# Modulation vectors summed along rows of transposed weights, and four PSUM banks for the second chunk of a joined output stage

## What is computed

```python
sc, sc_ctx = jax.nn.silu(c), jax.nn.silu(c_ctx)
for i in range(DEPTH):                                  # 2 layers
    m  = (sc @ w_mod[i] + b_mod[i]).reshape(B, N_MOD, D_MODEL)[:, :, None, :]
    mc = (sc_ctx @ w_mod[i] + b_mod[i]).reshape(N_MOD, D_MODEL)
    shift_m, scale_m, gate_m, shift_f, scale_f, gate_f = [m[:, k] for k in range(N_MOD)]
    h = modulate(rmsnorm_2(x, g_pre_mix[i]), shift_m, scale_m)
    ...
```

## Time and profile before

| what | value |
|---|---|
| median of 3 executions | 3549.88 us (3549.67 to 3550.25) |
| profiled execution | span 3547.7 us from first to last instruction (its own time is not given apart; the median lies 2.2 us above this span) |
| PE, PEld (weight load) | 3348.4 us (94%), 2947.4 us (83%) |
| DVE | 2189.7 us (62%) |
| ACT, POOL | 1734.8 us (49%), 1370.2 us (39%) |
| granted PE clock, mean | 0.971 of full speed |
| DMA | 337.33 MB, mean 95 GB/s |

### The profile page before, as it was taken

One profiled execution on the slowest core, in us unless ns is written; L12 is line 12 of the kernel. 1 busy time (PEld: TensorE's weight loads), 2 busy tenths in 40 slices (PEclk: granted clock), 3 DMA queues, 4 the chain that ended last, 5 costly groups with the idle time before them and its releaser, 6 DMA issues. The chain is left out here.

```text
span 3547.7 us, 57878 instructions
## 1 busy us (share of the span) xinstructions
PE 3348.4 (94%) x18421; PEld 2947.4 (83%) x18421; DVE 2189.7 (62%) x4470; ACT 1734.8 (49%) x4097; POOL 1370.2 (39%) x1781
## 2 busy tenths in 40 slices
PE   8899798999999999797999989999999889999999
PEld 7899587999999997686899868888788768888787
DVE  7467775555677776335888476656436775665335
ACT  2578123767777772333566363333334653333233
POOL 5465333555666773313222524444102224444000
PEclk9999899999999998898999989999999989999999
DMA  6211745111222114400000122222355212221464
GB/s 264 82 31 46 286 186 183 42 35 49 62 64 66 57 61 175 138 1 30 1 0 0 54 107 77 89 79 81 119 176 193 83 65 83 77 89 71 145 198 161
DMA packets 104142, 337.33 MB, mean 95 GB/s; under 512 B 11617, under 2 KB 40209, under 8 KB 90258
## 3 DMA queue, kind: packets, MB, share of 16 engines
q1 hardware_dynamic: 103954, 335.07, 27.3%
HBM read 273.13 MB, written 61.10 MB: 94 GB/s over the span
## 5 line engine op out<-in xcount | busy, mean ns | idle before, releaser
L2128 PE MATMUL ps<-down_high,hidden_high 128*128 128x512 f32 x688 | 269.3, 391 | 6.9 <-DVE hidden_low L2029 4.4
L2129 PE MATMUL ps<-down_low,hidden_high 128*128 128x512 f32 x688 | 268.0, 390 | 0.0
L2130 PE MATMUL ps<-down_high,hidden_low 128*128 128x512 f32 x688 | 268.0, 389 | 0.0
L2027 DVE TENSOR_TENSOR down_low<-down_raw,down_high 128x1024 fp32r<-128x1024 f32 x86 | 108.7, 1264 | 247.6 <-ACT down_high L1942 247.5
L2108 PE MATMUL ps<-columns_combined,up_high_even 128*128 128x512 f32 x616 | 242.8, 394 | 13.0 <-DVE columns_combined L2427 5.9
L2109 PE MATMUL ps<-columns_combined,up_high_even 128*128 128x512 f32 x616 | 241.8, 393 | 0.0
L2110 PE MATMUL ps<-columns_combined,up_low_even 128*128 128x512 f32 x616 | 241.6, 392 | 0.0
L2108 PE MATMUL ps<-columns_combined,up_high_odd 128*128 128x512 f32 x616 | 239.6, 389 | 0.0
L2109 PE MATMUL ps<-columns_combined,up_high_odd 128*128 128x512 f32 x616 | 239.6, 389 | 0.0
L2110 PE MATMUL ps<-columns_combined,up_low_odd 128*128 128x512 f32 x616 | 239.6, 389 | 0.0
L1137 ACT ACTIVATE masked_then_probs<-masked_then_probs,unit_rows 128x256 f32<-128x256 f32 (+1 forms) x512 | 229.2, 450 | 9.1 <-DVE unit_rows L1216 4.3
(11 more groups left out here) (440 smaller groups left out, 10131.9 us busy)
## 6 DMA issues: line engine op xcount, KB each, us to landing
up_raw<-in_w_up SPq DMA_DIRECT2D x44, 1024.0 KB, 4.8
down_raw<-in_w_down SPq DMA_DIRECT2D x88, 512.0 KB, 3.6
mod_weights_b<-in_w_mod SPq DMA_DIRECT2D x32, 1024.0 KB, 6.0
hidden_columns<-hidden SPq DMA_DIRECT2D x44, 512.0 KB, 2.6
hidden_columns<-hidden_columns SPq DMA_DIRECT2D x88, 256.0 KB, 3.9
w_raw<-in_w_in_b SPq DMA_DIRECT2D x24, 768.0 KB, 4.6
mod_weights<-in_w_mod SPq DMA_DIRECT2D x8, 2048.0 KB, 11.9
x_kept<-x SPq DMA_DIRECT2D x24, 512.0 KB, 2.7
```

The lines of the kernel that those rows point to most:

```text
L2128: nc.tensor.matmul(out, h_hi[to][:, t], down_hi[to][:, cols], start=begin, stop=False)
L2129: nc.tensor.matmul(out, h_hi[to][:, t], down_lo[to][:, cols], start=False, stop=False)
L2130: last = nc.tensor.matmul(out, h_lo[to][:, t], down_hi[to][:, cols], start=False, stop=(end and to == self.slot(h, f, s)))
```

## The change

- `w_mod` is laid out transposed: block b holds, for 128 output features on the partitions, the weights of all 1024 inputs in a row. There are 96 blocks of 128x1024. silu(c) and silu(c_ctx) are rows of 1024, copied to all partitions by a DMA (`c_rows`), with the SiLU on ACT (two operations of 128x1024 in the opening). The row of silu(c) stays in SBUF at a fixed place (`C_ROW_AT`).
- One `tensor_tensor_reduce` of DVE multiplies a block by the row and sums it into one column of `mod_sums`; its 128x1024 output (`unread`, two of them in turn) is not used. No transposes, no reductions, no wait on the operation just before, but on the one before that.
- Loads are pairs of blocks, 1 MB, three slots in the ring in every stage.
- Blocks by stage: opening 24, of which 16 for both vectors (40 operations); joined stage 40; second mixer's output product 32.
- Joined stage: `EARLY` = 16 blocks before `add(0, m)`, one block behind each tile of chunk 1 (at the end of the tile's work, behind `low`), the last 16 after `low(TILES - 1)`. Chunk 1 uses four banks (`m % 4`), and the gate columns' product waits for the additions only.
- `mixer_out` is written out by itself in place of `project`; x is loaded at its start and not after the split of the tokens. The two groups of products stand before the additions of chunk 0 and before those of chunk 1.

```diff
+class Modulation:
+    SLOTS = 3
...
+    def load(self, sp, q):
+        if q >= self.SLOTS:
+            sp.wait_ge(core.mod_sums.sem, core.mod_sums.at(self.before(2 * (q - self.SLOTS + 1))))
+        at = self.first + 2 * q
+        sp.dma_start(self.raw[:, q % self.SLOTS], self.w[at:at + 2].rearrange("b p n -> p b n")).then_inc(self.landed[q % self.SLOTS].sem, 16)
+
+    def products(self, dve, a, b):
...
+            for v in range(2 if n < self.both else 1):
+                i = self.before(n) + v
+                if i >= 2:
+                    dve.wait_ge(core.mod_sums.sem, core.mod_sums.at(i - 1))
+                dve.tensor_tensor_reduce(out=self.unread[:, i % 2], in0=self.raw[:, q % self.SLOTS, n % 2], in1=self.rows[v], scale=1.0, scalar=0.0,
+                                         op0=ALU.mult, op1=ALU.add, accum_out=self.sums[:, v, n:n + 1]).then_inc(core.mod_sums.sem, 1)
```

In `opening`:

```diff
-                side.sync(sp, 0)
+                for n in range(2):
+                    sp.dma_start(modulation.rows[n], I["c_rows"][n].partition_broadcast(P)).then_inc(core.beside0.sem, 16)
+                for q in range(3):
+                    modulation.load(sp, q)
                 sp.dma_start(X[:], I["x"][0].rearrange("(m p) n -> p m n", p=P)).then_inc(core.post_row.sem, 16)
...
-                side.sync(sp, 1)
+                for q in range(3, 8):
+                    modulation.load(sp, q)
                 for c in range(CHUNKS):
...
+                    for q in range(8, 0 if c else modulation.pairs):
+                        modulation.load(sp, q)
...
+                act.wait_ge(core.beside0.sem, core.beside0.at(32))
+                for n in range(2):
+                    act.activation(modulation.rows[n], modulation.rows[n], ACT.Silu).then_inc(core.expo.sem, 1)
...
-                side.pe(lambda m: pe.wait_ge(core.acc_used_act.sem, core.acc_used_act.at((CHUNKS - 1) * TILES + m + 1)))
```

In `out_and_gate`:

```diff
                 sp.dma_start(X[:], old).then_inc(core.ready2.sem, 16)
-                for q in range(SLOTS, 9):
-                    mod(q)
+                mods(3, 6)
                 split_done(KT)
                 load(3)
-                mod(9)
-                mod(10)
+                mods(6, 9)
...
-                    dve.tensor_tensor(X[:, m, cols], ps[:, m if c == 0 else m % 2, :], X[:, m, cols], ALU.add).then_inc(core.acc_used_dve.sem, 1)
+                    dve.tensor_tensor(X[:, m, cols], ps[:, m if c == 0 else m % 4, :], X[:, m, cols], ALU.add).then_inc(core.acc_used_dve.sem, 1)
...
-                early = 48
-                products(0, early)
+                modulation.products(dve, 0, EARLY)
...
                     add(1, m)
-                    if m >= 2:
-                        reduced(0, m - 2, 3 - m % 2)
-                    products(early + 2 * m, early + 2 * m + 2)
                     normed(m)
                     if m:
                         low(m - 1)
-                reduced(0, MODS - 2, 3)
+                    modulation.products(dve, EARLY + m, EARLY + m + 1)
                 low(TILES - 1)
-                reduced(0, MODS - 1, 4)
-                shifted(0)
-                products(KT * MODS, 2 * KT * MODS)
-                for n in range(MODS):
-                    reduced(1, n, n)
-                shifted(1)
+                modulation.products(dve, EARLY + TILES, modulation.blocks)
+                modulation.shift(dve)
...
-                    pe.wait_ge(core.acc_used_dve.sem, core.acc_used_dve.at(m + 1 if m < 2 else TILES + m - 1))
+                    pe.wait_ge(core.acc_used_dve.sem, core.acc_used_dve.at(m + 1 if m < 4 else TILES + m - 3))
...
-                            if k == 0 and m in (0, 1):
-                                pe.wait_ge(core.acc_used_dve.sem, core.acc_used_dve.at(2 * TILES - 1 + m))
-                            if k == 0 and m in (2, 3, 4):
-                                pe.wait_ge(core.mod_reduced.sem, core.mod_reduced.at(m + 4))
+                            if k == 0 and m < 4:
+                                pe.wait_ge(core.acc_used_dve.sem, core.acc_used_dve.at(TILES + m + 5))
```

The new `mixer_out`, DVE's part of it:

```diff
+                modulation.products(dve, 0, EARLY)
+                dve.wait_ge(core.ready2.sem, core.ready2.at(16))
+                add(0)
+                modulation.products(dve, EARLY, modulation.blocks)
+                modulation.shift(dve)
+                add(1)
```

More of the change, by code:

```diff
@@ L321, in _ @@
             def _(sp):
-                if side:
-                    side.sync(sp, 0)
-                if loads_for_next is not None:
-                    loads_for_next(sp)
-                if old is not None:
-                    if unsplit is not None:
-                        sp.wait_ge(core.lo_done.sem, core.lo_done.at(KT))
-                    sp.dma_start(*old).then_inc(core.ready2.sem, 16)
-                def stores(c):
-                    for m in range(mtiles):
-                        used, each, n = taken_by(m)
-                        sp.wait_ge(used.sem, used.at((c + 1) * each + n + 1))
-                        sp.dma_start(store(m, c), dest(m, c)).then_inc(core.loads.sem, 16)
@@ L338, in chunk @@
-                def chunk(c):
-                    for h in range(HALVES):
-                        sp.wait_ge(core.split.sem, core.split.at((c - 1) * KT + (h + 1) * KH))
-                        weights.load(sp, c, h)
-                    if side:
-                        side.sync(sp, c)
-                    if store:
-                        stores(c - 1)
-                each_chunk(sp, 1, chunk)
-                if store:
-                    stores(chunks - 1)
-                    sp.wait_ge(core.loads.sem, core.loads.at(16 * mtiles * chunks + 16))
+                sp.dma_start(X[:], old).then_inc(core.ready2.sem, 16)
@@ L365, in _ @@
-                splits(0, RING)
-                each_chunk(pool, 1, lambda c: splits(c, 0))
+                for n in range(RING, CHUNKS * KT):
+                    before, at = divmod(n - RING, KT)
+                    if at == KT - 1:
+                        pool.wait_ge(core.acc.sem, core.acc.at((before + 1) * TILES))
+                    else:
+                        pool.wait_ge(core.split_used.sem, core.split_used.at(before * (KT - 1) + at + 1))
+                    pool.nop(nofuse=True)
+                    weights.split(pool, n // KT, n % KT)
@@ L446, in project @@
-            if add and unsplit is not None:
-                @block.scalar
-                def _(act):
-                    split_high(act)
-    if side:
-        side.passed()
-    if store:
-        core.loads.passed(16 * mtiles * chunks + 16)
-    if old is not None:
-        core.ready2.passed(16)
-    if unsplit is not None:
-        core.hi_done.passed(KT)
-        core.lo_done.passed(KT)
-    core.raw0.passed(16 * chunks)
-    core.raw1.passed(16 * chunks)
-    core.split.passed(KT * chunks)
@@ L2630, in passed, with opening @@
             c.passed(each)
[L2633 removed]
+def opening(core, I, T, X, vec, vcol, nsink, c_row, row_factors, modulation, gate_rows):
     nc, (t_hi, t_lo) = core.nc, T
@@ L2858, in dve_end, with shift @@
+    def shift(self, dve):
+        core = self.core
+        dve.wait_ge(core.mod_sums.sem, core.mod_sums.at(self.before(self.blocks)))
         for v, out in enumerate(self.outs):
-            dve.tensor_tensor(out[:, cols], self.columns[:, v], self.shifts[:, cols], ALU.add)
+            n = self.both if v else self.blocks
+            cols = slice(self.first, self.first + n)
+            dve.tensor_tensor(out[:, cols], self.sums[:, v, 0:n], self.bias[:, cols], ALU.add)
     def passed(self):
-        core, n = self.core, self.chunks
@@ L2863, in passed @@
-        for c, count in ((core.ready0, 8 * n), (core.ready1, 8 * n), (core.up_used, n + 2), (core.turned, self.nv * n),
-                         (core.links_dve, self.nv * (KT + 1) * n)):
-            c.passed(count)
-def out_and_gate(core, T, unsplit, old, kept, weights, w_gate, norm_row, X, vector, w_mods, firsts, outs, shifts, gate_rows):
+        for s, c in enumerate(self.landed):
+            c.passed(16 * len(range(s, self.pairs, self.SLOTS)))
+        self.core.mod_sums.passed(self.before(self.blocks))
```

342 lines of the change are left out of this document (100 added, 242 removed).

## The result

| | before | after |
|---|---|---|
| median of the runs | 3549.78 us (3549.66 to 3550.25, 4 runs) | 3504.11 us (3501.53 to 3506.54, 4 runs) |
| profiled execution: its own time, its span | as shown above, 3547.7 us | 3506.54 us, 3504.4 us |
| ratio of the medians, 95% interval | | 0.9875, 0.9862 to 0.9887 |

The change makes the kernel 45.7 us faster. A second set of the same kernel, made later, gave 3504.24 (3502.24 to 3507.39).

What follows compares the result with a forecast made beforehand. The prediction took PE, busy 94% of the span, as the bound, so DVE's work pays only where PE or the next stage waits for it. Terms summed to -34.0 us, taking the median from 3549.9 to 3516; range 3510 to 3530.

Steps and rivals of the forecast that it cites:

- The second mixer: Second mixer up to its output product: the forecast had 0 change there.
- the new rhythm: Joined stage, chunk 1: product behind `low` makes DVE fall back until PE waits at some five tiles, +2.7 us (0 to 6).
- The price of one operation: The new DVE product over 1024 elements: 1.32 us alone, 1.76 beside POOL's splits, no way seen below 1.2.
- The opening: End of the opening: 32 transposes and 8 reductions go, and with them SP's 2.8 us wait, -2.8 us.
- The long wait: Joined stage, start of chunk 1: early products end at about 410 us, so PE's wait for DVE's addition goes, -18.0 us.
- the first rival: Joined stage: early products are late, PE waits up to 5 us, 8 to 15 us given back, 3524 to 3531; chance 0.25.
- Slow clock and the 2.9 us wait: Joined stage: full clock behind the long wait, -2.6 us; modulation-sum wait and slow clock behind it go, -5.5 us.
- The transposes that are gone from PE: Joined stage: eight groups of four transposes at 0.36 us each leave PE, -2.9 us.
- the joined stage's missing 2.9: Joined stage: forecast -28.6 us, measured -31.5, so 2.9 us more than forecast.
- The second output product: Second mixer's output product: the reductions at its end go, -2.6 us; x and the loads come in the other order.
- The half rate: Rival for the new DVE product: two SBUF inputs with accumulator run at half rate, +30 us in all, 3580; chance 0.12.

Runs made afterwards that it cites:

- the run with 40 MEMSETs: The kernel before with 40 MEMSETs of one column each on DVE in the opening: 3541.40 us, ratio 0.998.

## Why the prediction was wrong in size, point by point

Two steps failed. The second mixer was put at nothing, and 4.5 us came from it; and the new rhythm was put at +2.7 and cost 0.9. With the rhythm alone put right the forecast would have been 3514, within its range; with the second mixer's 4.5 us as well it is 3510, at the range's lower end, and some smaller terms below carry it out.

- *The price of one operation* (1.32 alone, 1.76 beside POOL): 1.21 alone, one every 1.15 us, and 1.96 on average beside POOL in the early part, one every 1.9. I had added the accumulator's read-out to the product, and the two overlap; the rate of one in 1.15 us lies even under the 1.2 below which I saw no way.
- *The opening* (-2.8): -2.4 in the profiled execution, -2.75 in its repeat. DVE was done at 94.0 us (forecast 86 to 103), and x landed at 41.4, not later than before. The wait that the forecast names went from 2.8 to 0.2. That the difference fits so well is partly luck, since the openings of repeats lie over a microsecond apart: 105.9 to 107.5 in four traces of the kernel before, 104.2 to 107.2 in eight with the changed opening.
- *The long wait* (-18.0): right, early products ended at 408.45 (forecast about 410). PE began chunk 1 at 410.64. From the last product to PE's end of chunk 0 were 1.9 us and not the 2.5 that I gave, and with the first addition in between 1.2, so the first rival was nearer than its chance suggested.
- *Slow clock and the 2.9 us wait* (-2.6 and -5.5): gone. The first slow clock was sized a little high: the 13 matmuls of the first stretch were busy 5.50 us, which gives 2.5, and from PE's first matmul of chunk 1 to its first row transposes the stage gained 2.3. The one behind the 2.9 us wait is not certain: the run with 40 MEMSETs had the wait without it.
- *A new rhythm in chunk 1* (+2.7, 0 to 6): **a step of the sum that failed.** The mechanism was right: DVE's step is longer than PE's, the lateness collects, and when the slack is used up PE waits at each tile. Its size was wrong. I took 5.6 us from the addition to the end of `low`, with a wait for the statistics as long as before; it is 435.81 - 430.22 = 5.59 in the tiles beside POOL's splits and 5.27 in the others (455.34 - 450.07), and the product adds 1.14 and not 1.3 to 1.8. So a step is 6.72 and then 6.40, for PE's own 6.33 (the run with the product moved back), and not 6.9 to 7.4. The slack was used up at the third tile, as forecast; PE lost 0.2 us there, 0.4 at the next tile and some 0.08 at each of the four behind it, where I had 0.3 to 0.9 at five. Only one of these is long enough to be listed as a wait (0.2 us). In all the rhythm cost 0.9 us: 45.20 us from the first to the last row transposes on PE, against 44.33. That is 1.8 of the joined stage's missing 2.9. With doubled products the same waits grow to 6.3 us.
- *The transposes that are gone from PE* (-2.9): low by 0.9. With them a tile's step on PE was 6.80 us on average, without them it is 6.33, so each group cost 0.47 and not the 0.36 between the rows' starts.
- *What I costed at nothing*: the second mixer, **the other step that failed.** I counted a removed operation by its time and its place in the chain, and not by its place in the program. 4.5 of the 9.3 us by which the spans' difference exceeds the sum came from there. The trace of before did show it: 3.3 and 2.9 us of DVE waiting for nothing visible, in a stage that I hadn't read since no instruction in it changes.
- *The second output product* (-2.6): -3.4 and, in the repeat, -3.1; x in the other order cost nothing, and PE had no wait between the chunks. The rest of the program differs by 1.7. Repeats of the changed kernel alone lie from 2093.5 to 2099.6 us there; but the four traces of kernels before have 2098.4 to 2101.0, some 2 us more on average, so a part of it may be real. Its cause stays open.
- *The half rate*: not so. Its consequence was worked out to 3580, for a measured 3583 with doubled products, if with the stages less well met than the sum. The Trainium skill's rule ("Vector Engine (DVE) Microarchitecture Reference", section "Points that are easy to get wrong") doesn't show for this operation: two fp32 inputs from SBUF with an accumulator take 1.21 us for 1024 elements, the same as a subtraction of 128x1024 with one input from PSUM and no accumulator (1.21 alone) in the same timeline.

The sum with these terms put right: -34.0 - 1.8 (rhythm) - 0.9 (transposes) - 4.5 (second mixer) = -41.2, against -43.3 in the profiled executions. The rest is the second output product (-0.8) and the unexplained -1.7 of the rest of the program, against +0.6 in the opening and the first mixer.

## What to carry to other kernels

A wait that is removed is worth its length plus the slow clock behind it, where there is one. A new step that is longer than another engine's costs nothing until its lateness has used up the slack, and from then on only the difference of the two steps at each tile (0.4 and then 0.08 us here): both steps have to be known to a tenth of a microsecond before their difference is priced. And a change of the number of instructions moves all later code: where an engine runs through loops and the trace shows idle time with no releaser, look there before and after, and compare stage by stage before crediting the change with all that the clock shows.

## What was not expected of the hardware

- The place of DVE's code is worth 4 to 5 us in one stage: 766.1, 765.8 and 765.1 us at instruction 1103, 759.8 to 761.7 at the five other places, and 100 instruction packets against 89 to 91.
- The multiply-and-sum with both inputs in SBUF and an accumulator takes 1.21 us for 1024 fp32 elements; beside POOL's splits it takes 1.62 and 2.30 in turn, and POOL's casts 1.61 for 0.61.
- The slow clock comes and goes between executions of one program, at the end of the first mixer (256.5 or 259.5 us). That is 3 of the up to 10 us by which the runs of one kernel lie apart (3544.43 to 3554.68), where the first four runs of before lay within 0.6; the rest of the spread is not explained, since only one execution of each run has a trace.
